# Gated RWKV-7 / gMLP block with a 32-expert FFN: the front of the kernel laid out with features on partitions and heads in both halves

## What is computed

```
h = rms_norm(x) ;  z = h @ w_in          # 3360 RWKV columns | u 1024 | v 1024 | gate A 1024 | gate B 1024
# RWKV-7: token shift, z = z + (shift(z) - z) * time_mix, then r, k, v, and three low-rank inputs
decay = exp(-exp(-softplus(-(w0 + tanh(zw) @ w_decay_up)) - 0.5)) ; a = sigmoid(a0 + za @ a_up)
g = sigmoid(zg) @ g_up ; kk = k * k_k / norm per head ; k = k * (1 + (a - 1) * k_a)
# per head (16 heads of 64), over the tokens:
state = state * w + (state @ -kk) (x) (kk * a) + v (x) k ;  y = state @ r
y_a = (group_norm(y) * gn_w + gn_b + sum(r * k * r_k) * v) * g
# gMLP in chunks of 128 tokens: tril(w_spatial) @ LN(gelu(v)) + b_spatial, times gelu(u)
x = x + (sigmoid(gate A + b) * y_a + sigmoid(gate B + b) * y_b) @ w_out
x = x + MoE(rms_norm(x))                 # top 4 of 32 experts, gate_up 1024x2048, down 1024x1024
y = rms_norm(x)
```

## Time and profile before

| | us |
|---|---|
| time before, median of 3 (lowest, highest) | 1411.14 (1403.87, 1412.0) |
| the profiled execution: its own time | 1405.91 |
| its span, first to last instruction | 1404.1 |
| busy PE, DVE, ACT, POOL | 1268.5, 373.8, 214.7, 20.2 |
| moved by DMA | 449.64 MB |

### The profile page before, as it was taken

One profiled execution on the slowest core, in us unless ns is written; L12 is line 12 of the kernel. 1 busy time (PEld: TensorE's weight loads), 2 busy tenths in 40 slices (PEclk: granted clock), 3 DMA queues, 4 the chain that ended last, 5 costly groups with the idle time before them and its releaser, 6 DMA issues.

```text
span 1404.1 us, 13973 instructions
## 1 busy us (share of the span) xinstructions
PE 1268.5 (90%) x5937; PEld 545.7 (39%) x5937; DVE 373.8 (27%) x643; ACT 214.7 (15%) x376; POOL 20.2 (1%) x37
## 2 busy tenths in 40 slices
PE   6899998999988999989988988998888999888886
PEld 5677544556744333323322222332222333222221
DVE  2588686322443110112000111201101121100002
ACT  2656411212111101000100000000000000000002
POOL 1000010000010000000000000000000000000000
PEclk9999999975586999999999999999999999999999
DMA  8342454330093899999999999999999999999995
GB/s 219 92 117 90 136 210 149 120 124 1 4 357 119 320 421 421 421 422 420 421 421 421 422 421 421 421 421 421 421 421 421 421 421 421 421 421 421 422 421 221
DMA packets 97364, 449.64 MB, mean 320 GB/s; under 512 B 8478, under 2 KB 35184, under 8 KB 48144
## 3 DMA queue, kind: packets, MB, share of 16 engines
q1 hardware_dynamic: 94592, 440.14, 78.0%
q0 software_dynamic: 2704, 8.54, 1.8%
HBM read 446.56 MB, written 2.10 MB: 320 GB/s over the span
## 4 chain that ended last, share of the span: by engine, by line
DMA 47%; PE 39%; DVE 7%; ACT 4%; issue 2%; SPq 1%; POOL 0%; DVEq 0%; ACTq 0%
DMA ring<-w_gate_up 44%; PE ps L1354 11%; PE ps L1374 4%; PE ps L1147 4%; PE ps L1343 3%; PE ps L1090 3%; PE ps L1289 2%; DMA ring<-w_down 2%; DVE prod L771 2%; PE ps L1268 2%; PE ps L1267 2%; DVE xl L772 1%; PE ps L1401 1%; PE ps L1241 1%; PE ps L1248 1%
## 5 line engine op out<-in xcount | busy, mean ns | idle before, releaser
L1354 PE MATMUL ps<-ring,xT 128*64 128x512 f32 x2048 | 469.3, 599 | 38.0 <-DMA ring<-w_gate_up 36.5
L1374 PE MATMUL ps<-ring,aT 128*64 128x512 f32 x1024 | 239.6, 600 | 41.9 <-DMA ring<-w_down 41.9
L1354 PEld LDWEIGHTS ps<-ring,xT 128*64 128x64 f32 x2048 | 137.5, 136 | 350.1 <-issue 273.9
L1043 DVE TENSOR_SCALAR gc<-ps 128x512 f32<-128x512 f32 x32 | 22.1, 690 | 680.4 <-PE ps L1354 680.4
L1374 PEld LDWEIGHTS ps<-ring,aT 128*64 128x64 f32 x1024 | 67.8, 136 | 210.5 <-issue 125.2
L1147 PE MATMUL ps<-wb,hT 128*128 128x512 f32 x256 | 112.2, 596 | 1.9 <-DVEq L256 1.9
L1090 PE MATMUL ps<-hT,wa 128*128 128x256 f32 (+1 forms) x432 | 99.7, 392 | 4.8 <-DVE hT L695 3.0
L1090 PEld LDWEIGHTS ps<-hT,wa 128*128 128x128 f32 (+1 forms) x432 | 82.9, 194 | 19.1 <-DVE hT L695 3.3
L657 ACT ACTIVATE sgm<-gc 128x512 f32<-128x512 f32 x32 | 20.2, 630 | 362.8 <-DVE gc L1043 362.8
L1147 PEld LDWEIGHTS ps<-wb,hT 128*128 128x128 f32 x256 | 48.2, 191 | 59.1 <-issue 57.0
L1401 PE MATMUL ps<-ysl,oht 64*128 64x512 f32 x256 | 64.5, 622 | 0.7 <-ACT ysl L649 0.7
(11 more groups left out here) (243 smaller groups left out, 848.5 us busy)
## 6 DMA issues: line engine op xcount, KB each, us to landing
ring<-w_gate_up SPq DMA_DIRECT2D x256, 1024.0 KB, 27.0
ring<-w_down SPq DMA_DIRECT2D x128, 1024.0 KB, 27.1
wb<-w_in SPq DMA_DIRECT2D x8, 2048.0 KB, 8.5
wa<-w_in SPq DMA_DIRECT2D x26, 512.0 KB, 3.9
wb<-w_out SPq DMA_DIRECT2D x2, 2048.0 KB, 9.5
xacc<-x SPq DMA_DIRECT2D x2, 512.0 KB, 4.0
bc<-b_gate POOLq DMA_DIRECT2D x2, 512.0 KB, 9.5
out<-xacc SPq DMA_DIRECT2D x2, 512.0 KB, 2.7
```

Of the source, the lines that this page charges most:

```text
L1354: last = mm(bank(GU_BANK + q, 0, 512, slice(64 * half, 64 * half + 64)), x_, w[:, D * half + 512 * q:D * half + 512 * (q + 1)], start=k == ...
L1374: last = mm(bank(DN_BANK, 0, 512, slice(64 * half, 64 * half + 64)), aT[:, c0:c0 + SLOTS], w[:, D * r + 512 * half:D * r + 512 * (half + 1 ...
```

## The change

The front is written anew; the experts' part is kept, with other buffer addresses. Features stay on partitions throughout, and of each pair of heads one lies in partitions 0 to 63 and one in 64 to 127.

- Stage A: the projections go k first (all eight), then r and v of each c. ACT's copy scales by 1 - mix (`unshifted`), and DVE adds the shifted part straight from PSUM, one operation. Key norms are 8 matmuls with one column, the root is taken once for all, and `spread_norms` spreads the reciprocals with one matmul. `products` makes 16 chunk products of 64x128 and 24 transposing matmuls of 64x64, each in the quarter of the array that its head's rows and columns give.
- Between: 4 chunks for v, 8 tiles for u (each 8 matmuls of 128x256), the inverse by outer products, its round trip issued by ACT, one `with_x11` and one `with_x22` for all.
- The recurrence: sums over state and over values are separate matmuls of 64x64, 16 a group, heads alternating between two quarters of the array. The 16 gate tiles and the gate's low-rank products (`gate_lora`) are put between the groups (`FILL`).
- After it: the group norm's centring is folded into the values, its variance is a matmul with one column for each head, `project_out` reads the merged values directly, without `turn_block`.
- The meetings of all engines are dropped. The ring's first 9 loads wait for `y_done`, 5 for `out_done`, 1 for `h2_ready`.

```diff
+        FILL = [[2, 1, 1], [2, 1, 1], [2, 1, 1], [2, 2, 0]]
...
-        SLOT_AT = ([FRONT + 8 * KB + 8 * KB * i for i in range(8)] + [FRONT]
-                   + [WBUF + 16 * KB, WBUF + 24 * KB, WBUF, WBUF + 8 * KB, WBUF + 32 * KB, WBUF + 40 * KB])
+        SLOT_AT = ([SREG + 8 * KB * i for i in range(8)] + [VREG] + [WREG + 8 * KB * i for i in range(4)] + [XREG, HREG])
...
+            sp.wait_ge(sm["y_done"], NCH)
+            for n in range(9):
                 load(n, pieces[n])
...
+            sp.wait_ge(sm["out_done"], 2 * TB)
+            for n in range(9, 14):
+                load(n, pieces[n])
             sp.wait_ge(sm["h2_ready"], 2)
             load(14, pieces[14])
...  ACT
+            act.wait_ge(sm["nrm_done"], KT)
+            act_(small[:, 200:232], bank(6, 0, SYS), ACT.Sqrt).then_inc(sm["nrm_root"], 1)
...
+            value_gelu(0)
+            turned_copies(KT - 1)
+            act.wait_ge(sm["gram_out"], 2 * KT)
+            for hh in range(2):
+                for k in range(2):
+                    lo, l0 = HD * hh + 32 * k, 64 * hh + 32 * k
+                    act.dma_start(scr_a[l0:l0 + 32].rearrange("l s t -> s l t"), GBs[lo:lo + 32, :, 32 * k:32 * k + 32]).then_inc(sm["lanes_st"], 16)
+            value_gelu(1)
+            act.wait_ge(sm["lanes_st"], 64)
+            act.wait_ge(sm["bv_ready"], KT)
+            act.dma_start(al[:, :], scr_a.rearrange("l s t -> l (s t)")).then_inc(sm["lanes_ld"], 16)
...  DVE, the inverse
-            for t in range(1, 32):
-                pr = prod[:, 0:t * t].rearrange("p (n s) -> p n s", n=t)
-                link(V.tensor_tensor(pr, xl_v[:, 0:t, 0:t], al_v[:, 0:t, t].unsqueeze(1).to_broadcast([P, t, t]), MUL))
-                link(V.tensor_reduce(xl_v[:, 0:t, t], pr, AX.X, ADD))
+            for s in range(31):
+                n, m_ = s + 1, 31 - s
+                pr = prod[:, 0:n * m_].rearrange("p (n t) -> p n t", n=n)
+                link(V.tensor_tensor(pr, xl_v[:, 0:n, s].unsqueeze(2).to_broadcast([P, n, m_]),
+                                     al_v[:, s, s + 1:32].unsqueeze(1).to_broadcast([P, n, m_]), MUL))
+                link(V.tensor_tensor(xl_v[:, 0:n, s + 1:32], xl_v[:, 0:n, s + 1:32], pr, ADD))
             dve.sem_inc(sm["lanes_done"], 1)
...  PE, stage A
             for c in range(KT):
+                project(RV + 2 * c)
                 if c == 0:
+                    key_norms(KT - 1)
+                spread_norms(c)
+                project(RV + 2 * c + 1)
                 if c:
                     products(c - 1)
...  PE, products
+                for q in range(NCH):
+                    for w in range(2):
+                        for hh in range(2):
+                            last = mm(bank(4 + w, q * P, P, hrows(hh if w == 0 else 1 - hh)), part(w, q, hh), AR_v[hrows(hh), c, q, :], start=True, stop=True)
...  PE, between
+            value_chunk(2)
+            value_chunk(3)
+            for t in range(6):
+                tile(t)
+            with_x11()
+            tile(6)
+            with_x22()
+            tile(7)
+            for g in range(GROUPS):
+                spatial(g)
...  PE, one group of the recurrence, and their order
+                for c, hh in heads:
+                    last = mm(bank(5, c * HD, HD, hrows(hh)), GB_v[hrows(hh), c, q, 0:CH], rb[hrows(hh), of_head(c)], start=True, stop=True)
+                last.then_inc(sm["u_done"], 1)
...
+            rows_of_values(0)
+            for q in range(NCH):
+                if q:
+                    rows_of_state(q)
+                fill(q, 0)
+                if q:
+                    spread_deviation(q - 1)
+                solved(q)
+                if q < NCH - 1:
+                    rows_of_values(q + 1)
+                    state_of_values(q)
+                outputs_of_values(q)
+                fill(q, 1)
+                if q < NCH - 1:
+                    state_of_solved(q)
+                outputs(q)
+                fill(q, 2)
+                if q < NCH - 1:
+                    variances(q)
...
-            turn_block(ysb, 0, "m_ready", 0, "m_ps")
-            for half in range(2):
-                project_out(0, half)
-            turn_block(ysb, 1, "m_ready", 1, "m_ps")
+            project_out(0, 0, range(0, 4))
+            variances(NCH - 1)
+            project_out(0, 0, range(4, KT))
+            spread_deviation(NCH - 1)
+            project_out(0, 1, range(KT))
```

More of the change, by code:

```diff
@@ new lines, in build @@
+        VC = at("VC", VREG, NCH * KT * HD)
+        hT = at("hT", HREG, KT * T)
+        XM = at("XM", XREG, KT * T)
+        m = Map(QREG, END)
+        sg = m.take("sg", 2 * T)
+        plast = m.take("plast", SYS)
+        FRONT = QREG + 2304
+        m1 = Map(FRONT, END)
+        sw = m1.take("sw", KT * T)
+        sa = m1.take("sa", KT * T)
+        zk = m1.take("zk", KT * T)
+        upw = m1.take("upw", D)
+        zl = [m1.take(f"zl{i}", T) for i in range(3)]
+        zr = [m1.take(f"zr{b}", T) for b in range(2)]
@@ L453, in _, with unshifted @@
             own("xrms")
[L454 to L457 removed]
+            def unshifted(n, dst, rows=P):
                 act.wait_ge(sm["proj_done"], n + 1)
[L459 to L465 removed]
@@ L679, in _ @@
             for b in range(2):
-                for i in range(3):
-                    last = V.memset(zp[b][i][:, 0:1], 0.0)
-            last.then_inc(sm["pads"], 1)
-            own("pads")
+                V.memset(dec[b][:, 0:NCH * (CH + 1):CH + 1], 1.0).then_inc(sm["ones_set"], 1)
             dve.wait_ge(sm["xrms"], 2)
@@ new lines, in products @@
+                last.then_inc(sm["vc_done"], 1)
+                pe.wait_ge(sm["q_ready"], c + 1)
+                if c:
+                    pe.wait_ge(sm["bv_ready"], c)
+                mm(bank(3, 0, T), C("headones"), qb[b][:, :], start=True, stop=True).then_inc(sm["bonus_done"], 1)
+            for n in range(4):
+                project(n)
+            lora_up(0)
+            lora_up(1)
+            for c in range(1, KT):
+                project(KEYS + c)
+                key_norms(c - 1)
+                if c + 1 < KT:
+                    lora_up(c + 1)
@@ new lines, in tile @@
+            def tile(t):
+                j = t // 2
+                pe.wait_ge(unit_sem("f", j), unit_filled("f", j))
+                if t < 2:
+                    pe.wait_ge(sm["v_out"], t + 1)
+                else:
+                    pe.wait_ge(sm["f_out"], t - 1)
+                wv = unit((2 * j + 4) % 8, 2).rearrange("p (k n) -> p k n", k=KT)
+                for k in range(KT):
+                    last = mm(f_slot(t), wv[:, k, P * (t % 2):P * (t % 2) + P], hv[:, k, :], start=k == 0, stop=k == KT - 1, skip_group_check=True)
+                last.then_inc(sm["f_done"], 1)
@@ new lines, in spatial, with gate_lora @@
+            def spatial(g):
+                pe.wait_ge(sm["vn_ready"], 2)
+                if g < 2:
+                    pe.wait_ge(sm["v_out"], 3 + g)
+                else:
+                    pe.wait_ge(sm["sp_out"], g - 1)
+                for tb in range(TB):
+                    last = mm(bank(2 + g % 2, tb * P, P), vsb[:, tb * D + g * P:tb * D + (g + 1) * P], wst[:, g * P:(g + 1) * P], start=True, stop=True)
+                last.then_inc(sm["sp_done"], 1)
+            def gate_lora(c):
+                pe.wait_ge(sm["gu_in"], 32)
+                pe.wait_ge(sm["lo_act"], 3)
+                if c == 0:
+                    pe.wait_ge(sm["sp_out"], GROUPS)
+                else:
+                    pe.wait_ge(sm["ga_ready"], c)
+                o = bank(2, 0, T)
+                mm(o, gu1[:, c * P:(c + 1) * P], sg[:, 0:T], start=True, stop=False)
+                mm(o, gu2[:, c * P:(c + 1) * P], sg[0:32, T:2 * T], start=False, stop=True).then_inc(sm["gl_done"], 1)
@@ new lines, in variances, with spread_deviation @@
+            def variances(q):
+                pe.wait_ge(sm["ysq_out"], q + 1)
+                if q:
+                    pe.wait_ge(sm["yn_ready"], q)
+                else:
+                    pe.wait_ge(sm["sp_out"], GROUPS)
+                for c, hh in heads:
+                    last = mm(bank(3, c, 1, hrows(hh)), ysq[hrows(hh), c * CH:(c + 1) * CH], C("ones", hrows(hh))[:, 0:1], start=True, stop=True, skip_group_check=True)
+                last.then_inc(sm["var_done"], 1)
+            def spread_deviation(q):
+                pe.wait_ge(sm["d_ready"], q + 1)
+                mm(bank(3), C("headones"), dg[:, :], start=True, stop=True).then_inc(sm["rb_done"], 1)
@@ new lines, in project_out @@
+            def project_out(tb, half_, ks):
+                pe.wait_ge(sm["m_ready"], 2 * tb + 2)
+                for k in ks:
+                    if tb == 0 and half_ == 0:
+                        pe.wait_ge(unit_sem("o", k), unit_filled("o", k))
```

(12 more changed lines are left out.)

1175 lines of the change are left out of this document (566 added, 609 removed).

## The result

The changed kernel takes 1350.37 us (median of 4, 1346.54 to 1351.0) against 1409.12; the ratio of the two is 0.9586, 95% interval 0.9554 to 0.9618. The forecast of 1384 had the sign and the range right (1350 to 1423, at its very edge) and the size wrong: 59 us came instead of 27. The profiled execution has a span of 1344.7 us where the sum gave 1380.0.

The account below looks back on a forecast made before the run. Before the experts' fixed 948.6 us, PE's work, its clock and the chain around the inverses were taken to bound. Experts starting at 431.4 gave 1380.0 of span; 1.8 around it and half of 5.2 made 1384, range 1350 to 1423.

Parts of the forecast that it names:

- the unit price: Small matmuls of stage A and recurrence: 48 ns per 64x64 instruction, between ends of 35 and 64 ns.
- the 43 ns of a weight load: Small matmuls: loading 64 columns of weights takes 43 ns, which overlapping two quarters doesn't shorten.
- One term: Recurrence: three variances at 4.6 us, added to 31 groups of small matmuls at 47.6 us.
- The clock, 6 us: Recurrence: 6 us added to 118 us at full clock, because small matmuls alone had run at 0.90 and 0.50.
- Gate tiles and low-rank products: Recurrence: 16 gate tiles at 55.4 us and `gate_lora` at 7.7 us.
- The DRAM trips: Around the inverse: load 0.6 + 3.57 us, store about 3.1, loads back 4.86 behind 1.6 of issue.
- corner products: Before the recurrence: `with_x11` at 4 x 1.12 us and `with_x22` at 4.5 us.
- only the start of the experts counts: Experts' part: unchanged at 948.6 us, so each microsecond won before it is one of the whole.
- DVE's and ACT's savings in stage A: Stage A: their removed work lay beside PE's, so its removal was costed at nothing.
- the inverse: Before the recurrence: outer products with operands along rows take 22.8 us, before 39.8.
- Rival 1: Small matmuls: only the issue limit is left, 35 ns everywhere and no clock loss; 30 less, 1354; chance 0.20.
- Rival 2: Small matmuls: the quarters do not overlap, 64 ns an instruction; 39 more, 1423; chance 0.20.

Follow-up runs that it names:

- the first experiment: Changed kernel with each recurrence group's heads reordered, first the eight of the lower half, then the eight of the upper, so neighbours share a quarter: 1377.04 us.
- The run with both edits: Changed kernel with recurrence heads ordered lower half first, then upper, and all 16 gate tiles ahead of the first solve: 1401.47 us.
- the filled hole: Changed kernel with GpSimd issuing the inverses' DRAM trip and u tiles, spatial products and a gate tile filling PE's wait: 1337.95 us, again 1337.64 us.

## Why the prediction was wrong

**The step that failed is the unit price.** "For a new 64x64 instruction the ends are 35 and 64 ns; I take 48." It costs 29 to 34, 30 on average. The 35 came from 32x32 matmuls in one quarter, and I took it for the issue limit. It is none: the same kind of matmuls, alternating between two quarters, took 2.14/128 = 17 ns after (L1203, at a clock of 1.00; the 3.62 of L1195 is at 0.50). The Trainium skill, "TensorE: Matmul & The Clock Gate", section "Wait — 56ns, not 53.3ns?", puts the least distance of two matmul starts at about 25 ns. The 29 ns would fit it, the 17 ns per instruction do not, and the measurement decides. The windows of the changed kernel over its two groups of corner products, PE alone (busy us, PEclk, DMA, GB/s):

```profile
212.90:216.50 3.60, 3.60 (x129) 0.50 0.02 5
...
222.10:224.30 2.20, 2.20 (x130) 1.00 0.00 0
```

And I held up the 43 ns of a weight load as a cost that overlap doesn't shorten. It does: the group after has 64 columns of weights too. The overlap itself is shown by the first experiment. The other end was misread as well: the 64 ns of the earlier trace rows is L1258, tiles of 128 rows by 64 columns, two quarters and not one; in one quarter the first experiment gave 51 to 57.

**One term was counted twice.** The recurrence has 28 groups of 64x64 matmuls and three of variances; the 31 groups and 992 instructions of the forecast hold the variances already, and it adds 4.6 us for them once more. The trace after has 896 + 96 instructions.

What this was worth: the 992 instructions cost about 30 us where the sum had 47.6 + 4.6. That is 17.6 us of price and 4.6 of counting. In stage A, `products` took 2.9 instead of 4.4, seven times, and the key norms 0.56 instead of 0.77, eight times, 12 us. So the price makes 30 of the 35 us between the two spans.

**The clock, 6 us, came out at nothing.** I charged it since small matmuls had run at 0.50. Those matmuls lay in one place of the array at a time, between stretches of turns between tile sizes. The run with both edits shows 0.50 again for a single quarter without wide work; the changed kernel has neither, nor the turns.

**Against these stand misses of the other sign.** Gate tiles and low-rank products cost 3.5 more; the first of them behind small matmuls takes 0.2 us more, which I had not priced. The DRAM trips took 5.1 and 6.2 us, and 9.9 behind 1.6 of issue, where I had 4.2, 3.1, and 4.9 behind 1.6: 9 more. A load of 1 MB beside the store is part of it, as the run with the old inverse shows. Shorter work before the inverse (16.7 instead of 19.2) and cheaper corner products (5.8 instead of 9) made good most of that, so the stretch to the recurrence took 87.3 instead of 84. The merge took 2 more and the experts 2 less.

**What was right:** that only the start of the experts counts (948.6 against 946.6), that DVE's and ACT's savings in stage A lie under PE (its chain of waits there is PE's but for 1.3 us), the inverse, and the order of the stages. Rival 1 (1354) named the overlap and the full clock, at 0.20, and came within 4 us; but its 35 ns was no limit, and it too counts the variances twice and has the DRAM trips too short, so that it came so close is in part luck. It should still have been the forecast: rows 3 showed an overlap of the full factor of two, and nothing but my floor stood against it. Rival 2 is refuted. What I didn't see at all is that 42 us were to be had without the change, by one edit to the kernel before: the turn between tile sizes, which I had not priced, was in plain sight in its chain of waits.

What stays open: why the load of the inverses back took 9.9 us where the kernel before had its two loads, issued by GpSimd, landed in 5.3 at most. The issuing engine, the other traffic and the cut into four loads changed together. Nor did I try how the gain of the filled hole divides between its several edits.

## What to carry to other kernels

Before a stage of small matmuls is laid out anew, look at the order of its instructions: neighbours in different quarters of the array overlap, neighbours in one quarter don't, and turns between two tile sizes cost most of all. One loop split gave 42 us here. When pricing small matmuls, take the lower end from two that may overlap, not from a row where they can't, and look at the clock of the row first.

## What had not been expected of the hardware

- Matmuls of 64 rows by 64 columns in two quarters, written to the same PSUM bank, ran at 29 ns an instruction; in one quarter at 51 to 57. Those of 32 by 32 in two quarters ran at 17 ns.
- Turns between 128-row and 64-row tiles cost 130 ns an instruction at full clock and 200 at half, against 67 grouped, and the clock stayed low over the wide matmuls behind them.
- A PE that was busy 34 of 35 us ran at 1.2 GHz throughout when its matmuls were small and all in one quarter; in two quarters in turn it kept 0.95.
- 4096 pieces of 128 bytes from DRAM back into SBUF, issued by ScalarE beside other loads, took 8.6 to 9.9 us, against 5.1 for the load in whole rows.
- A store of 0.5 MB from SBUF to DRAM took 2.7 us alone and 6.2 with a load of 1 MB beside it.
